# A gated DeltaNet stage: the learning rate as a logarithm in the decay exponent, and the order of work on four engines

## What is computed

```
beta = sigmoid(b_logit);  g = -exp(a_log) * softplus(a_logit + dt_bias)
g = cumsum(g) within a chunk
decay  = exp(where(incl, g[:, None] - g[None, :], -inf))
a_mat  = (k * beta) @ k.T * where(strict, decay, 0)
sol    = triangular_solve(I + a_mat, [v * beta, k * beta * exp(g)])
qk     = (q @ k.T) * decay
# over the chunks:  v_new = u - w @ s;  o = q*exp(g) @ s + qk @ v_new
#                   s = s * exp(g_last) + (k * exp(g_last - g)).T @ v_new
o = rmsnorm(o_fwd + o_bwd) * norm_w * silu(z)
```

## Time and profile before

| | |
|---|---|
| median of three runs (3055.65, 3055.91, 3061.22) | 3055.91 us |
| the profiled execution | 3061.32 us |
| its span on the core | 3059.6 us |
| PE busy | 2888.3 us, 94% of the span |
| DVE, ACT, POOL busy | 1299.4, 1072.4, 1206.5 us |
| mean granted TensorE clock | 0.968 |

### The profile page before, as it was taken

One profiled execution on the slowest core, in us unless ns is written; L12 is line 12 of the kernel. 1 busy time (PEld: TensorE's weight loads), 2 busy tenths in 40 slices (PEclk: granted clock), 3 DMA queues, 4 the chain that ended last, 5 costly groups with the idle time before them and its releaser, 6 DMA issues. The chain is left out here.

```text
span 3059.6 us, 38554 instructions
## 1 busy us (share of the span) xinstructions
PE 2888.3 (94%) x15219; PEld 2356.4 (77%) x15219; DVE 1299.4 (42%) x1953; ACT 1072.4 (35%) x1829; POOL 1206.5 (39%) x805
## 2 busy tenths in 40 slices
PE   6999999999999969578778999999999999999998
PEld 5878787877888846477667887878888888888887
DVE  5233233321479949666564353322233232232323
ACT  4241313243044539455544122332333333333232
POOL 2222122121123320423421433466666666766663
PEclk9999999999999979878798999999999999999999
DMA  4434233343545357210103546332322333332331
GB/s 114 165 132 140 80 102 102 100 132 94 184 148 176 120 189 249 80 44 31 73 31 126 179 141 208 105 100 93 102 91 91 103 96 124 97 97 91 114 110 58
DMA packets 239571, 352.78 MB, mean 115 GB/s; under 512 B 32928, under 2 KB 186272, under 8 KB 239392
## 3 DMA queue, kind: packets, MB, share of 16 engines
q1 hardware_dynamic: 239392, 350.32, 35.2%
HBM read 263.71 MB, written 96.36 MB: 118 GB/s over the span
## 5 line engine op out<-in xcount | busy, mean ns | idle before, releaser
L102 PE MATMUL pj_acc<-u_hi,pj_w_hi 128*128 128x512 f32 x1464 | 576.6, 394 | 10.6 <-DVE u_lo L823 10.6
L2763 DVE TENSOR_TENSOR x_tm<-m_ps,x_tm 128x512 f32<-128x512 f32 x384 | 265.0, 691 | 745.8 <-PE m_ps L104 745.8
L104 PE MATMUL pj_acc<-u_hi,pj_w_lo 128*128 128x512 f32 x1464 | 571.9, 391 | 0.0
L103 PE MATMUL pj_acc<-u_lo,pj_w_hi 128*128 128x512 f32 x1464 | 571.7, 391 | 0.0
L551 POOL TENSOR_TENSOR pj_w_lo<-pj_w_raw,pj_w_hi 128x1024 fp32r<-128x1024 f32 x61 | 159.2, 2610 | 722.0 <-ACT pj_w_hi L600 722.0
L2645 POOL TENSOR_TENSOR m_lo<-gate,held 128x1024 fp32r<-128x1024 f32 x96 | 237.8, 2500 | 270.0 <-ACT held L2562 270.0
L102 PEld LDWEIGHTS pj_acc<-u_hi,pj_w_hi 128*128 128x128 f32 x1464 | 275.9, 188 | 85.7 <-issue 18.2
L104 PEld LDWEIGHTS pj_acc<-u_hi,pj_w_lo 128*128 128x128 f32 x1464 | 276.1, 189 | 58.2
L103 PEld LDWEIGHTS pj_acc<-u_lo,pj_w_hi 128*128 128x128 f32 x1464 | 276.2, 189 | 56.2
L102 PE MATMUL m_ps<-held 128*128 128x512 f32 x768 | 299.7, 390 | 2.4 <-DVEq L2744 2.4
L102 PE MATMUL m_ps<-held,m_h_hi 128*128 128x512 f32 x768 | 299.5, 390 | 0.0
(11 more groups left out here) (308 smaller groups left out, 4939.8 us busy)
## 6 DMA issues: line engine op xcount, KB each, us to landing
gate<-in_w_mlp_dram SPq DMA_DIRECT2D x48, 1024.0 KB, 5.4
gate<-in_w_mlp_dram SPq DMA_DIRECT2D x96, 512.0 KB, 3.7
proj<-pj_stage SPq DMA_DIRECT2D x61, 768.0 KB, 3.4
pj_w_raw<-in_w_in_dram SPq DMA_DIRECT2D x61, 512.0 KB, 5.2
gate<-proj SPq DMA_DIRECT2D x24, 768.0 KB, 4.4
mo_w_raw<-in_w_out_dram SPq DMA_DIRECT2D x48, 256.0 KB, 2.9
rpb_bias<-pj_shut SPq DMA_DIRECT2D x48, 192.0 KB, 3.1
rpb_bias<-rpb_near SPq DMA_DIRECT2D x24, 384.0 KB
```

Of the source, the lines that this page charges most:

```text
L102: pe.matmul(out, w_hi, x_hi, start=first, stop=False)
L103: pe.matmul(out, w_hi, x_lo, start=False, stop=False)
L104: return pe.matmul(out, w_lo, x_hi, start=False, stop=last)
L2763: dve.tensor_tensor(xt, ps2[:, q % 4], xt, ALU.add).then_inc(added, 1)
```

## The change

**Rates.** A new column tile `lnb` holds ln(max(beta, 1e-30)) of all heads. It is made once at the start of attention (one DVE operation, one Ln on ACT over 128x96). `decay_columns` adds one operation, `sb = col + lnb`, and the strict decays are exponentials with `sb` in the place of the column, so that beta is in them. `scores` is then one operation over 128x512 a group, with the constant -1, where there were four over 128x128.

**Place.** ACT takes 4 of the copies into `un` (direction 0, tiles 0 and 2; behind the first narrow operation alone), DVE keeps 12 copies, now of one count each by semaphores `un0_d0`, `un0_d1`, `un0_late`. Of these DVE's first eight, direction 1, come first and direction 0, tile 1, last.

**Order.** POOL: the inclusive masks stand ahead of the two multiplications by the queries; for the last head nothing changes there. ACT: EG of the next head moves from the inverse steps 0 and 2 to recurrence steps 5 and 6 of the head before (for the first head ahead of the cut); the cut moves ahead of the output copies of step 2; the inclusive exponentials move from steps 1 and 3 to 3 and 4. DVE: out_sum behind the first two evictions, columns from k = 6 to k = 1, the cut behind the state update of step 2, the third pair of queries from step 4 to 5, the gate of z from step 5 to 6. Token-major turns and their multiplications keep one step of distance, the norm steps move by two.

```diff
-def decay_columns(dve, c, cols, col, ncol, cx, gq):
+def decay_columns(dve, c, cols, col, ncol, cx, gq, lnb, sb):
     c.link(dve.tensor_copy(col, cols))
+    c.add(dve.tensor_tensor(sb, col[:, 0:2], lnb, ALU.add))
     c.add(dve.tensor_scalar(ncol, col, -1.0, None, ALU.mult))
...
+            dve.tensor_scalar(lnb[:], cols[:, :, 2:4], 1e-30, None, ALU.max).then_inc(d_rates, 1)
...
+            act.activation(rates, rates, ACT.Ln).then_inc(d_rates, 1)
...
-SQUARES_AT, ROOT_AT, EG_AT, CEXP_AT = 1, 5, (0, 2), 10
-LENGTHS_AT, MEAN_AT, DIAG_AT, SPREAD_AT, NORM_AT, GATE_AT = 2, 3, 5, (7, 9, 11), (8, 10, 12), 12
-TURN_AT = (0, 3, 6, 9, 11, 13)
-TOKEN_AT = ((1, 2), (4, 5), (7, 8), (10, 11), (12, 13), (14, 15))
-COLUMNS_AT = 6
-INCL_AT = {8: 4, 11: 5, 13: 0, 15: 1}
+SUM_AT, SQUARES_AT, LENGTHS_AT, MEAN_AT, ROOT_AT, DIAG_AT = 0, 3, 4, 5, 7, 7
+SPREAD_AT, NORM_AT, GATE_AT = (9, 11, 13), (10, 12, 14), 14
+COLUMNS_AT, CEXP_AT = 1, 9
+TURN_AT = (0, 3, 6, 9, 12, 15)
+TOKEN_AT = ((0, 1), (3, 4), (6, 7), (9, 10), (12, 13), (15, 16))
+INCL_AT = {8: 4, 10: 5, 12: 0, 14: 1}
...
-INCL_END = {1: 3, 3: 2}
+INCL_END = {3: 3, 4: 2}
...
-QK_IN = {0: (4, 5), 1: (0, 1), 4: (3, 2)}
-CUT_IN, WIDE_IN, ZTANH_IN, ZGATE_IN, SPREAD_IN = 2, 3, 4, 5, 7
+QK_IN = {0: (4, 5), 1: (0, 1), 5: (3, 2)}
+CUT_IN, WIDE_IN, ZTANH_IN, ZGATE_IN, SPREAD_IN = 2, 3, 4, 6, 7
+EG_IN = (5, 6)
...
             for i in range(HEADS):
-                decayed_queries(i)
                 if i + 1 == HEADS:
+                    decayed_queries(i)
                     continue
...
                     masked(qk2[:, (i + 1) % 2, n], i + 1, n, incl).then_inc(S["mask_i"], 1)
+                decayed_queries(i)
...
-                exponentials(i, n, am[:, n], col2, -1.0, S["exp_s"])
+                exponentials(i, n, am[:, n], sb2, -1.0, S["exp_s"])
...
-                act.wait_ge(S["spread"], 2 * i + 2)
+                act.wait_ge(S["spread"], 2 * i + 1)
...
+                for q in Q32:
+                    act.copy(by_direction(un, q, 0)[:, 0:NTB:2, :, q], compact(c1, q, 0)[:, 0:NTB:2]).then_inc(S["un0_d0"], 1)
+                act.wait_ge(S["spread"], 2 * i + 2)
...
+                    if more and step == CUT_IN:
+                        cut_blocks(i + 1)
...
+                        if step in EG_IN:
+                            row_decays(i + 1, EG_IN.index(step))
...
-                for j in range(4):
-                    last = dve.scalar_tensor_tensor(am[:, n, j], ps[:, 4 + 2 * (GRAMS.index(tg) % 2), j],
-                                                    ncol2[:, i % 2, 2 + d, 4 * tg + j:4 * tg + j + 1], decays[:, j], ALU.mult, ALU.mult)
-                last.then_inc(S["am_done"], 1)
+                dve.scalar_tensor_tensor(am[:, n], ps[:, 4 + 2 * (GRAMS.index(tg) % 2)], -1.0, decays, ALU.mult,
+                                         ALU.mult).then_inc(S["am_done"], 1)
...
+                for q in Q32:
+                    dve.tensor_copy(by_direction(un, q, 0)[:, 1:2, :, q], compact(c1, q, 0)[:, 1:2]).then_inc(S["un0_late"], 1)
...
-                if i:
-                    out_sum(i - 1)
...
+                        if k == SUM_AT:
+                            out_sum(i - 1)
```

More of the change, by code:

```diff
@@ L1040, in attention @@
     strict, incl, join = masks
-    y2, gq, kb, col2, ncol2, cx2 = ahead
+    y2, gq, kb, col2, ncol2, cx2, lnb, sb2 = ahead
     dd0 = kb[:].rearrange("p (a j) n -> p a j n", j=4)
@@ L1259, in delta_decay @@
                 act.wait_ge(d_masked, a + 1)
-                act.activation(dd0[:, a, j], dd0[:, a, j], ACT.Exp, bias=(col2, ncol2)[q][:, 0, d, t:t + 1],
+                act.activation(dd0[:, a, j], dd0[:, a, j], ACT.Exp, bias=(sb2, ncol2)[q][:, 0, d, t:t + 1],
                                scale=(-1.0, 1.0)[q]).then_inc(d_exp, 1)
+            rates = lnb[:].rearrange("p h d t -> p (h d t)")
+            act.wait_ge(d_rates, 1)
+            act.activation(rates, rates, ACT.Ln).then_inc(d_rates, 1)
             for u in range(U + 1):
@@ L1607, in incl_decays, with row_decays @@
                 exponentials(i, n, qk2[:, i % 2, n], ncol2, 1.0, S["exp_i"])
+            def row_decays(i, d):
+                act.wait_ge(S["mask_s"], i * NG6 + NG6)
+                act.wait_ge(S["mask_i"], i * NG6 + NG6)
+                act.wait_ge(S["cols_in"], i + 1)
+                act.activation(gq[:, i % 2, d], gq[:, i % 2, d], ACT.Exp).then_inc(S["eg"], 1)
             def cut_blocks(i):
@@ L1612, in cut_blocks @@
                 if i:
-                    act.wait_ge(S["un0"], i * 16)
+                    act.wait_ge(S["un0_late"], i * 4)
                     act.wait_ge(S["tn0_pool"], i * 4)
@@ L1620, in place @@
             def place(i):
-                act.wait_ge(S["spread"], 2 * i + 2)
+                act.wait_ge(S["spread"], 2 * i + 1)
                 if i:
+                    act.wait_ge(S["new_mm"], (i - 1) * 24 + 4 * BOTH)
                     act.wait_ge(S["u_mm"], i * NS)
@@ L1654, in main @@
                         out_root(i - 1)
[L1655 to L1660, removed]
                     if k == CEXP_AT and more:
@@ L1696, in _ @@
             act.sem_inc(S["exp_i"], NG6)
+            for d in range(2):
+                row_decays(0, d)
             cut_blocks(0)
@@ L1750, in main @@
                         if k < NG6:
-                            pe.wait_ge(S["un0"], i * 16 + (4, 8, 4, 8, 12, 16)[k])
+                            done_by, count = (("un0_d0", 4), ("un0_d1", 4), ("un0_d0", 4), ("un0_d1", 4), ("un0_d1", 8), ("un0_late", 4))[k]
+                            per = 8 if done_by == "un0_d1" else 4
+                            pe.wait_ge(S[done_by], i * per + count)
                         else:
@@ L1913, in narrow, with place @@
                 dve.wait_ge(S["spread"], 2 * i + 2)
-            def place(i, first):
-                if i:
[L1918 to L1922, removed]
+            def place(i):
+                for t, free in ((slice(1, NTB), 4 * BOTH), (slice(0, 1), 24)):
+                    if i:
+                        dve.wait_ge(S["new_mm"], (i - 1) * 24 + free)
+                    else:
+                        dve.wait_ge(S["cleared"], 4)
                     for q in Q32:
-                        dve.tensor_copy(by_direction(un, q, d)[:, t, :, q], compact(src, q, d)[:, t]).then_inc(S["un0"], 1)
+                        dve.tensor_copy(by_direction(un, q, 1)[:, t, :, q], compact(c2, q, 1)[:, t]).then_inc(S["un0_d1"], 1)
+                for q in Q32:
+                    dve.tensor_copy(by_direction(un, q, 0)[:, 1:2, :, q], compact(c1, q, 0)[:, 1:2]).then_inc(S["un0_late"], 1)
             def token_major(i, n, d):
@@ L1942, in prepare @@
                     scores(i, n)
-                if part == CUT_IN:
-                    cut_blocks(i)
                 for n in QK_IN.get(part, ()):
@@ L1948, in prepare @@
                     narrow(i)
-                    place(i, True)
             def main(i, more, c, nxt):
-                if i:
-                    out_sum(i - 1)
                 for k in range(NS):
@@ L2000, in main @@
                             dve.tensor_copy(st[:, j], ps[:, j, 2]).then_inc(S["st_ev"], 1)
+                    if more and step == CUT_IN:
+                        cut_blocks(i + 1)
                 if more:
-                    place(i + 1, False)
+                    place(i + 1)
                 c.end()
@@ L2007, in _ @@
             dve.memset(ps[:, 0:2], 0.0).then_inc(S["blank"], 1)
-            dve.sem_inc(S["chain"], 8)
-            chains[0].n = 8
+            dve.sem_inc(S["chain"], 9)
+            chains[0].n = 9
             dve.sem_inc(S["cols_in"], 1)
@@ L2012, in _ @@
                 prepare(0, part, chains[0])
-            place(0, False)
+                if part == CUT_IN:
+                    cut_blocks(0)
+            place(0)
             for i in range(HEADS - 1):
```

24 lines of the change are left out of this document (12 added, 12 removed).

## The result

The changed kernel takes 3065.51 us (median of 12 runs, 3061.82 to 3070.19), the kernel before 3056.95 beside it. The ratio is 1.0026, with an interval from 1.0017 to 1.0035: 8.6 us slower. The forecast was 3.6 us faster. The measured time lies in the range, and its size is that of rival C (8 to 11 slower). The profiled execution has a span of 3065.3 us against 3059.6, so it shows 5.7 of the 8.6: the profiled execution of the kernel before was 4.4 above its median, that of the changed kernel 1.5.

A forecast was written before the change was run, and what follows sets the result against it. Chains between engines were taken to bound the DeltaNet, no engine being full. Terms -2.35 + 0.5 + 1.0 - 1.5 + 1.2 + 0.5 - 2.9 = -3.6 us gave 3052.3, range 3035 to 3069.

The forecast's parts named there:

- rival C: Starts of heads 0 to 2: columns and copies hold PE and the clock falls there; +8.1 to +11 us, 3067; chance 0.24.
- POOL against DVE: Starts of heads: DVE operations in SBUF alone get through one at a time between POOL instructions; columns' hold +8.3 us.
- Rival A: Starts of heads: DVE's copies keep POOL out, so placing isn't delayed; sum -14.4 us, 3041; chance 0.14.
- scores, cut and shared place: Scores -2.35 us in head 0's preparation; earlier cut -1.0 and ACT's copies -0.6, together -1.6 at heads 1 to 3.
- Rival D: Scores: the operation over 128x512 is no cheaper than four; -1.2 us in all, 3054.7; chance 0.43 together with the forecast.
- the give-back in heads 1 and 2: Heads 1 and 2: start -1.6, columns' hold +8.3, given back 8.1 us; -1.4 to +3.6, +0.5 taken for each.
- head 3: Last head: POOL's multiplications meet two DVE copies, +3.9 to +6.9, a spread +1.0; -3.5 to +1, -1.5 us taken.
- the gain from the clock: End of inverses: a high clock at the first Gram matrices saves 1.44 us; 0 to -5.8, two heads taken, -2.9.
- rival B: Later half of inverses: the clock stays high with fewer gaps at turns; -12 us, 3040; chance 0.19.
- Head 0: First head: DVE's copies make U's first eviction 4.9 to 9.4 us late, 6.3 given back; +0.5 taken.
- Attention and recurrence: ACT's moved EG and exponential +0.4 us at each of three heads, +1.2; table loads in attention +0.5.

## Why the prediction was wrong, step by step

**Right: POOL against DVE.** The mechanism and its size came as written. Copies in head 0: 15.5 us for 12 (the eviction behind them waited for the end of POOL's 14.3). Columns in heads 1 and 2: PE held for 9.02 and 10.17, forecast 8.3. One DVE operation per POOL instruction was read from masks of 1.23 and carried over to multiplications of 3.43; 3.44 to 3.46 bears that out. Rival A, that DVE's copies keep POOL out, falls: they went one at a time in heads 0 and 3.

**Right: scores, cut and shared place.** Forecast -2.35 and -1.6 a head. The preparation alone gave -2.6. The idle time ahead of a head's first S fell from 5.0 to 2.3; in heads 1 and 2 the second S now waits 0.9 for DVE's copies, so -1.8 a head is left. Rival D (no cheaper operation) falls with 1.29 for 2.16.

**Failed: the give-back in heads 1 and 2.** The prediction set 8.1 us of gains against a hold of 8.3, chose +0.5 a head, and it came out at +4.8 and +3.6, past its high end of +3.6 in head 1. The windows of the four heads, from first S to first S (the last to the merge; columns as in the windows above), show what kind of time that is. Before:

```profile
1282.73:1372.20 89.47, 72.34 (x816) 64.27 (x817) 58.11 (x140) 47.73 (x144) 35.64 (x48) 0.82 0.05 17
1372.20:1468.95 96.75, 78.74 (x846) 67.81 (x847) 62.99 (x148) 52.02 (x149) 39.71 (x48) 0.82 0.16 59
1468.95:1567.13 98.18, 78.06 (x846) 67.32 (x847) 62.65 (x148) 51.66 (x148) 37.05 (x48) 0.85 0.15 56
1567.13:1650.95 83.82, 68.43 (x798) 59.16 (x799) 43.70 (x99) 37.75 (x98) 9.54 (x3) 0.89 0.16 51
```

and after:

```profile
1276.12:1362.11 85.99, 68.00 (x817) 60.25 (x817) 63.51 (x119) 49.30 (x149) 35.71 (x49) 0.87 0.02 7
1362.11:1463.64 101.53, 78.80 (x847) 68.59 (x847) 69.32 (x127) 53.09 (x153) 36.99 (x49) 0.83 0.14 54
1463.64:1565.44 101.80, 77.43 (x847) 67.62 (x847) 69.78 (x127) 53.04 (x153) 36.99 (x49) 0.84 0.15 55
1565.44:1656.72 91.28, 73.14 (x798) 62.93 (x799) 50.59 (x99) 36.28 (x99) 8.55 (x4) 0.80 0.17 58
```

Length less busy time of PE is its idle time: it rose by 4.7 us in head 1 and by 4.3 in head 2, while PE was busy as long as before at the same clock. The gains did come: the waits at turns, 4.2 and 5.8 us in these two heads, went, and turns alone gave 11.4 us in a run by themselves. The step that failed is the balance: the waits that the change's own tables bring were put at nothing in these heads. Gate and last turn come so late that PE waits 2.75 and then 1.2 at the end of each of the two inverses, 4 us a head that the prediction has only as +1.0 in head 3; and the hold was 9.0 and 10.2 for 8.3.

The lower clock did not add to this. In the changed kernel it is low right behind PE's idle time, 0.50 from 1380 to 1396, of which two windows:

```profile
1384.00:1388.00 4.00, 4.00 (x23) 3.88 (x21) 1.46 (x3) 0.00 (x0) 0.00 (x0) 0.50 0.00 0
1388.00:1392.00 4.00, 4.00 (x44) 3.49 (x44) 0.00 (x0) 1.10 (x3) 0.00 (x0) 0.50 0.02 4
```

In the kernel before it was 0.50 in the later half of the same inverse instead, from 1400 to 1424. So the low stretch moved to the head's start, as rival C has it, without costing these heads more. C's price was the high ends of heads 0 to 2; that its 8 to 11 us is the size that was measured is luck, since it had head 0 at +3.1 and head 3 at -1.5, where -3.5 and +7.5 were measured.

**Failed: head 3.** Forecast -1.5, measured +7.5. Of the two ends for the copies, +3.9 and +6.9, the nearer was taken; PE waited 6.76, since the second product S needs the first four copies, and two of these stood behind a multiplication each (3.47 and 3.39). With what was given back, PE's idle time rose by 2.8. The larger part is its busy time, 73.1 for 68.4 at a clock of 0.80 for 0.89, which the prediction had nowhere; the same instructions ran in 85.53 in the run with the columns at step 6. Why the clock was low here stays open.

**Failed: the gain from the clock.** -2.9 was taken for two heads that would reach the first Gram products at the higher level. In the changed kernel the 16 products of head 2 took 3.39 as before:

```profile
1520.77 3.39 PE L1753 MATMUL dn_ps<-dn_yn 128*128 128x128 f32 x16 [1.21 <-DVE dn_kb L1950]
```

The wait for the last turn stands right ahead of them. Over the four heads PE was busy for 297.6 us before and 297.4 after, so this term was 0, and rival B falls with it. B also read PE as full at the lower level from one window; in the next one, 1308 to 1312, it was busy for 2.48 of 4 us.

**Head 0: shorter, by a clock that the change is not shown to have moved.** Forecast +0.5, measured -3.5. Its copies were as late as worked out, and PE's idle time rose by 0.9, although 2.4 went at the next head's start. But PE was busy for 68.0 instead of 72.3: the clock was 1.00 from 1300 to 1316, where it had been 0.50 from 1304 to 1328. In the run with the logarithm alone head 0 was as short without any of the moves, and in the run with the columns at step 6 the clock was 0.50 from 1312 to 1332 and the head 8 us longer. Why it stayed high is not settled; as a gain of the change it is luck.

**Attention and recurrence.** The two loads of tables cost nothing that shows: ACT made them while it waited for the first scores anyhow,

```profile
1093.51 1.28 ACT L1268 ACT_TABLE_LOAD   x1 [4.87 <-PEq L78]
1094.81 0.28 ACT L1268 ACTIVATE dn_lnb<-dn_lnb 128x96 f32<-128x96 f32 x1
1095.11 1.28 ACT L1276 ACT_TABLE_LOAD   x1
```

with the Ln 0.02 behind the first load, the second load 0.02 behind the Ln, and 3.49 us of waiting for the scores behind the second. The Trainium skill, page "ScalarE: Activation LUTs", section "What ACT_TABLE_LOAD costs", counts 2.66 for a switch with its drain; no drain shows here either, and by the rows the term was 0, not +0.5. The recurrences of heads 0 to 2, from the start of their first ks product to that of their last outputs, took 32.85, 33.16 and 34.44 against 32.87, 32.86 and 32.88: the moves on ACT cost 0.3 at most in the first two, and the third has a stretch at a clock of 0.57 near 1544.

Of the sum, then, the costs of POOL against DVE were right to about 2 us in heads 0 to 2 and 3 too small in head 3. The error was to offset them with gains of the same size: the four heads were forecast at -1.7 us with recurrence and clock, and measured at +12.4, all of it idle time of PE. The gains at the turns were real, but the change's own tables took most of them back at the end of the inverses, and the gain from the clock did not come.

## What to carry to other kernels

When an operation on one engine is made to start earlier, look at what it idled beside: POOL's wait for the exponentials was what let DVE's small SBUF operations through, and an added wait for those operations (28 us faster than before) was worth more than the earlier start. Short operations on the critical chain belong ahead of long ones on the engine that shares their path, and the shared path is found by looking for a short operation that takes as long as its neighbour's instruction. Here the costs that were read from rows as waits came out nearer than the give-backs did; for each give-back name what is late next at that very place.

## What the runs showed of the hardware that was not expected

A short DVE operation on SBUF took as long as the POOL instruction that it stood beside, one for one: 12 to 48 columns a row need 0.16 to 0.18 us alone, 1.19 to 1.30 beside masks of 1.23, and 3.44 to 3.46 beside multiplications of 3.43. A longer one, out_sum, took 2.66 for 1.76. DVE operations that read PSUM were not held in the same stretch (COPY_PREDICATED 0.73 beside the masks, as alone). POOL pays little for it: six masks took 7.41 alone and 8.94 with out_sum and two columns between them.

The same instructions in the same order took 91.28 and 85.53 us in head 3 of two kernels that differ only in heads 0 to 2, at mean clocks of 0.80 and 0.87. Whether what went before or only the execution makes that difference is not shown, as each kernel has one trace, and executions of one kernel lay up to 15 us apart. Differences of a few us in one head say little without the clock of that head, and PE's idle and busy time, beside them.
